# Key and receptance projections in three fp32r passes, a quarter of the value projection moved, rotation tables moved to GpSimd

## What is computed

```python
h = rms_norm(x, norm_g)
dx = jnp.pad(h, ((0, 0), (1, 0), (0, 0)))[:, :-1] - h
xr, xw, xk, xv, xa, xg = (h + dx * mu[i] for i in range(6))
r = xr @ w_r
k = xk @ w_k
v = xv @ w_v
...
o = wkv7_scan(rh, decay, kh, vh, -kk, kk * ah)
mean = jnp.mean(o, axis=-1, keepdims=True)
var = jnp.mean(jnp.square(o - mean), axis=-1, keepdims=True)
o = (o - mean) * lax.rsqrt(var + LNX_EPS)
o = o.reshape(Bn, Sn, Dn) * lnx_g.astype(f32) + lnx_b.astype(f32)
y = (o + bonus.reshape(Bn, Sn, Dn)) * g.astype(f32)
return y.astype(x.dtype) @ w_o, v_first
```

## Time and profile before

| | |
|---|---|
| median of 3 runs | 973.1 us (972.88 to 975.23) |
| the profiled execution | 973.55 us, its span 971.8 us |
| PE busy | 949.0 us (98%), 6740 matmul records |
| weight loads (PEld) | 826.7 us (85%) |
| DVE busy | 675.8 us (70%) |
| ACT busy | 449.0 us (46%) |
| POOL busy | 85.4 us (9%) |
| mean granted PE clock | 0.996 |
| the time mix | from the start to about 285 us of the span |
| first feed-forward layer, attention, second feed-forward layer | to about 478, 754 and 970 us |

### The profile page before, as it was taken

The page is one execution under the profiler, slowest core; times in us unless marked ns, Lnnn a source line. Parts: engine busy times, 40 slices in busy tenths (PEclk is TensorE's granted clock), DMA queues, the critical chain, the costliest instruction groups (busy, mean ns, idle before and its releaser), DMA issues.

```text
span 971.8 us, 17678 instructions
## 1 busy us (share of the span) xinstructions
PE 949.0 (98%) x6740; PEld 826.7 (85%) x6740; DVE 675.8 (70%) x1278; ACT 449.0 (46%) x717; POOL 85.4 (9%) x66
## 2 busy tenths in 40 slices
PE   8999999999999999999998999999999999999998
PEld 6778778787778888888898999999998798888887
DVE  7864766658647666666697788888878666666665
ACT  3323324224224444444446566666666554444442
POOL 0201000001010000000022121122112000000000
PEclk9999999999999999999999999999999999999999
DMA  9410320501514767666377555445544147666661
GB/s 300 141 58 1 113 75 1 174 13 26 150 44 129 198 192 194 194 194 194 107 255 211 149 145 159 134 124 157 144 143 134 23 139 227 184 191 184 187 185 58
DMA packets 195127, 136.85 MB, mean 141 GB/s; under 512 B 7279, under 2 KB 185967, under 8 KB 194941
## 3 DMA queue, kind: packets, MB, share of 16 engines
q1 hardware_dynamic: 195068, 136.03, 47.9%
HBM read 134.96 MB, written 1.05 MB: 140 GB/s over the span
## 4 chain that ended last, share of the span: by engine, by line
PE 62%; issue 24%; DVE 8%; POOL 5%; ACT 1%; DMA 1%; POOLq 0%; SPq 0%; DVEq 0%
PE wide L459 32%; PE bank L459 28%; POOL gsm L1910 4%; DVE work L1354 3%; DVE work L1357 2%; DVE x L1354 1%; DMA x<-in_x 1%; DVE wsp L1354 0%; DVE work L1641 0%; PE bank L482 0%; POOL small L1910 0%; ACT work L1028 0%; PE bank L557 0%; DVE wmix_low L1354 0%; DVE am L1354 0%
## 5 line engine op out<-in xcount | busy, mean ns | idle before, releaser
L459 PE MATMUL bank<-wpj,hkq 128*128 128x384 f32 x1152 | 215.8, 341 | 0.9 <-ACT once L1028 0.5
L459 PEld LDWEIGHTS bank<-wpj,hkq 128*128 128x128 f32 x1152 | 198.8, 189 | 5.1 <-issue 1.5
L459 PE MATMUL wide<-hsp,wsp 128*128 128x256 f32 (+2 forms) x1120 | 193.3, 329 | 0.0
L459 PEld LDWEIGHTS wide<-hsp,wsp 128*128 128x128 f32 x1120 | 172.3, 190 | 23.0 <-DVE hsp L1354 0.6
L1354 DVE TENSOR_TENSOR wsp<-ring,wsp 128x1024 fp32r<-128x1024 f32 (+1 forms) x88 | 150.7, 1752 | 4.2 <-ACT wsp L1028 4.2
L1028 ACT ACTIVATE wsp<-ring 128x1024 fp32r<-128x1024 f32 (+1 forms) x88 | 130.3, 1485 | 20.9 <-PE wide L459 14.0
L1354 DVE TENSOR_TENSOR wpj<-ring,wpj 128x1536 fp32r<-128x1536 f32 x48 | 84.2, 1754 | 21.6 <-ACT wpj L1028 21.6
L459 PE MATMUL bank<-wsp,asp 128*128 128x512 f32 x396 | 98.1, 392 | 0.0
L1910 POOL TENSOR_TENSOR gsm<-gsm,mhalf 128x6 f32<-128x6 f32 (+1 forms) x40 | 63.3, 1616 | 310.9 <-DVE gsm L1833 212.6
L459 PEld LDWEIGHTS bank<-wsp,asp 128*128 128x128 f32 x396 | 71.7, 189 | 13.1
L1028 ACT ACTIVATE wpj<-ring 128x1536 fp32r<-128x1536 f32 x48 | 71.2, 1484 | 22.0 <-PE bank L459 15.5
(11 more groups left out here) (253 smaller groups left out, 1163.2 us busy)
## 6 DMA issues: line engine op xcount, KB each, us to landing
ring<-in_f_w_gu SPq DMA_DIRECT2D x88, 512.0 KB, 5.9
ring<-in_w_kv SPq DMA_DIRECT2D x96, 256.0 KB, 3.5
ring<-in_f_w_down SPq DMA_DIRECT2D x44, 512.0 KB, 3.7
ring<-in_b_w_q SPq DMA_DIRECT2D x48, 256.0 KB, 3.5
wmix<-in_a_w_k SPq DMA_DIRECT2D x4, 1024.0 KB, 7.9
wmix<-in_a_w_r SPq DMA_DIRECT2D x4, 1024.0 KB, 10.0
wmix<-in_a_w_v SPq DMA_DIRECT2D x4, 1024.0 KB, 5.3
wmix<-in_a_w_o SPq DMA_DIRECT2D x4, 1024.0 KB, 5.3
```

What stands on the lines that cost most here:

```text
L459: return pe.matmul(o, a, b, start=start, stop=stop)
```

## The change

- The key projections of groups 1 to 3 and the receptance projections of groups 1 to 3 become three-pass products (`project_parts`). Group 0 keeps float32.
- High parts on ACT: the mixed inputs `xk` and `xr` once in group 0; the key columns (`kw_hi`) and receptance columns (`rw_hi`) in every group with a next one. Low parts on DVE: `xk` and `xr` in two halves each in group 0; in every group with a next one the two halves of the key columns behind levels 1 and 2, and those of the receptance columns behind the last copies of X, ahead of the output weights'.
- PE computes three quarters of the receptances ahead of `turn_output`, and one behind the sums of squares. The second quarter of the values moves from behind the matrices to between `turn_norms` and `product_o`.
- DVE makes `y_lo` ahead of the receptance products (`receptances`). In the last group `gu_lo` moves behind the two copies that PE waits for.
- SP's order: the output rows of a group are loaded behind the next group's receptance columns and ahead of its value columns, so that the key columns no longer stand behind `pe_wo`.
- The rotation tables are made by POOL, behind the inverse roots that it makes for the join, and DVE waits for all 12.
- In `heads`, `mean_squares(1, 0)` goes ahead of `half_lo(p, 5)` on DVE; in the last pair ACT makes `half_hi(p, 5)` and the square ahead of a piece of the output weights.

The diff, without a count (`it * 2` to `it * 6` in `product_o`), context and blank lines; 12 spaces of indentation are taken off:

```diff
@@ -358,29 +358,35 @@
-def load_mix(it):
-    for i, free in ((1, "pe_k"), (0, "pe_r"), (2, "pe_v")):
-        if it is not None:
-            sp.wait_ge(S(free), it)
-        c0 = 0 if it is None else it * 256
-        sp.dma_start(wmix[:, i, :].rearrange("p (k n) -> p k n", k=KT),
-                     cols[i][:, :, bass.ds(c0, 256)]).then_inc(s_wm[i], 16)
-        if it is None and i == 1:
-            load_second(c0)
-            sp.dma_start(cst[:, P:NCONST], ins["const"][:, P:NCONST]).then_inc(s_const, 16)
-    if it is not None:
-        sp.wait_ge(S("pe_z"), it * 2)
-        sp.wait_ge(S("pe_g"), it)
-        load_second(it * 256)
-        sp.wait_ge(S("pe_wo"), it * 4)
-    sp.dma_start(wmix[:, 3, :].rearrange("p (n d) -> p n d", n=2),
-                 wo_rows[0 if it is None else it]).then_inc(s_wm[3], 16)
-load_mix(None)
+def load_columns(i, it):
+    sp.dma_start(wmix[:, i, :].rearrange("p (k n) -> p k n", k=KT),
+                 cols[i][:, :, bass.ds(it * 256, 256)]).then_inc(s_wm[i], 16)
+def load_out(it):
+    sp.dma_start(wmix[:, 3, :].rearrange("p (n d) -> p n d", n=2), wo_rows[it]).then_inc(s_wm[3], 16)
+load_columns(1, 0)
+load_second(0)
+sp.dma_start(cst[:, P:NCONST], ins["const"][:, P:NCONST]).then_inc(s_const, 16)
+load_columns(0, 0)
+load_columns(2, 0)
+load_out(0)
 load_gain(1, ins["f_norm_g"][0])
 for it in range(1, NGRP):
-    load_mix(it)
+    sp.wait_ge(S("pe_k"), it)
+    load_columns(1, it)
+    sp.wait_ge(S("pe_r"), it)
+    load_columns(0, it)
+    if it > 1:
+        sp.wait_ge(S("pe_wo"), it * 4 - 4)
+        load_out(it - 1)
+    sp.wait_ge(S("pe_v"), it)
+    load_columns(2, it)
+    sp.wait_ge(S("pe_z"), it * 2)
+    sp.wait_ge(S("pe_g"), it)
+    load_second(it * 256)
+sp.wait_ge(S("pe_wo"), NGRP * 4 - 4)
+load_out(NGRP - 1)
@@ -596,8 +602,9 @@
             if v == 0:
-                pe.wait_ge(s_wm[1], it * 16 + 32)
-            project(7, 1, xk, "pe_k", [v])
+                pe.wait_ge(S("dve_x_lo"), 2)
+                pe.wait_ge(S("dve_mix_lo"), it * 6 + 2)
+            project_parts(7, 1, kw_hi, (xk_hi, xk_lo), "pe_k", [v])
         else:
@@ -616,13 +623,15 @@
         second_rank(it)
-    pe.wait_ge(s_wm[0], it * 16 + 16)
     if behind:
-        project(4, 0, xr, "pe_r", (0, 1))
+        pe.wait_ge(S("dve_x_lo"), 4)
+        pe.wait_ge(S("dve_mix_lo"), it * 6 - 2)
+        project_parts(4, 0, rw_hi, (xr_hi, xr_lo), "pe_r", (0, 1, 2))
         turn_output(it)
         sums_of_squares()
-        project(4, 0, xr, "pe_r", (2, 3))
+        project_parts(4, 0, rw_hi, (xr_hi, xr_lo), "pe_r", [3])
     else:
+        pe.wait_ge(s_wm[0], 16)
         pe.wait_ge(S("dve_mix"), 1)
@@ -637,6 +646,7 @@
         turn_norms()
+        project(6, 2, xv, "pe_v", [early - 1])
         pe.wait_ge(S("act_sa"), it + 1)
@@ -656,9 +666,6 @@
                         m.then_inc(S("pe_mats"), 1)
-    if behind:
-        project(6, 2, xv, "pe_v", [early - 1])
@@ -1102,6 +1109,10 @@
         A(tg[0:LG - P, 1, :], bank[3][0:LG - P, 0:T], ACT.Sigmoid).then_inc(S("act_lora"), 1)
+        act.wait_ge(S("dve_xk"), 2)
+        A(x_hi[:, 1, :], xk.rearrange("p k t -> p (k t)"), ACT.Copy).then_inc(S("act_x_hi"), 1)
+        act.wait_ge(S("dve_mix"), 1)
+        A(x_hi[:, 0, :], xr.rearrange("p k t -> p (k t)"), ACT.Copy).then_inc(S("act_x_hi"), 1)
     act.wait_ge(S("pe_k"), it + 1)
@@ -1133,11 +1144,17 @@
             A(M[:, 4 * c + h:4 * c + 4:2, 2:4, :], bank[MK[h]].rearrange("p (u m t) -> p u m t", u=2, m=2), ACT.Copy).then_inc(S("act_mats"), 1)
+    if ahead:
+        act.wait_ge(s_wm[1], it * 16 + 32)
+        A(kw_hi, wmix[:, 1, :], ACT.Copy).then_inc(S("act_mix_hi"), 1)
     act.wait_ge(S("pe_v"), it + 1)
...
     A(bPn.rearrange("p n i -> p (n i)"), bank[4][:, 256:512], ACT.Copy).then_inc(S("act_kn"), 1)
+    if ahead:
+        act.wait_ge(s_wm[0], it * 16 + 32)
+        A(rw_hi, wmix[:, 0, :], ACT.Copy).then_inc(S("act_mix_hi"), 1)
     if ahead:
@@ -1330,8 +1347,8 @@
     if B: copy_o(0); copy_p(1, 0); copy_p(1, 1)
+    if X: half_hi(p, 5); square(1, 1)
     if X and not follow: wo_high(4, last + 8)
-    if X: half_hi(p, 5); square(1, 1)
     if X and follow: half_hi(p + 1, 0)
@@ -1548,18 +1565,13 @@
     def low_key_weights(h):
-        dve.wait_ge(S("act_kw_hi"), it + 1)
+        dve.wait_ge(S("act_mix_hi"), it * 3 + 1)
     def low_query_weights():
-        dve.wait_ge(S("act_rw_hi"), it + 1)
+        dve.wait_ge(S("act_mix_hi"), it * 3 + 2)
-    def low_output_weights():
-        dve.wait_ge(S("act_mix_hi"), it * 1 + 1)
@@ -1619,13 +1631,16 @@
         decayed_keys()
-        receptances()
         dve.wait_ge(S("act_y_hi"), it)
         low_part(y_lo[:, :, :], yT[:, :, :], y_hi[:, :, :], "dve_y_lo")
+        receptances()
         unit_keys()
...
         invert_norms()
+        dve.wait_ge(S("act_x_hi"), 1)
+        dve.wait_ge(S("pe_k"), 1)
+        low_half("xk", 0)
         unit_keys()
@@ -1635,6 +1650,7 @@
         q.mark(dve.tensor_copy(pl[:, :, :], par[:, two, lg:lg + 2]))
+        low_half("xk", 1)
     if behind:
@@ -1658,6 +1674,10 @@
             add_output(it, [2, 3])
+        if not behind and c == 0:
+            dve.wait_ge(S("act_x_hi"), 2)
+            dve.wait_ge(S("pe_r"), 1)
+            low_half("xr", 0)
     for l in range(1, LEVELS - 1):
@@ -1676,6 +1696,8 @@
                 m.then_inc(S("dve_U"), 1)
+        if ahead and l in (1, 2):
+            low_key_weights(l - 1)
         if l == 3:
@@ -1686,18 +1708,24 @@
     q.mark(m)
-    if not ahead:
-        gu_lo(0, 0, 0)
     for h in range(2):
...
         dve.tensor_copy(Xc[HD:P, 4 * h:4 * h + 4, :], bank[h][HD:P, 0:256].rearrange("p (u t) -> p u t", u=4)).then_inc(S("dve_X"), 1)
-    if ahead and behind:
-        low_output_weights()
+    if not ahead:
+        gu_lo(0, 0, 0)
+    if not behind:
+        low_half("xr", 1)
+    if ahead:
+        low_query_weights()
+        dve.wait_ge(S("act_mix_hi"), it * 3 + 3)
+        low_half("ow", 0)
+        if behind:
+            low_half("ow", 1)
     dve.wait_ge(S("pe_S"), it + 1)
...
     m.then_inc(S("dve_S"), 1)
-    norm_output(it + 1, 0, None if behind else low_output_weights)
+    norm_output(it + 1, 0, None if behind else lambda: low_half("ow", 1))
 group(0, behind=False)
@@ -1809,17 +1837,7 @@
-dve.wait_ge(s_qkg, 32)
-for w in range(2):
-    for r in range(RT):
-        cosr = C("cos")[:, r * HD:(r + 1) * HD].rearrange("p (o d) -> p o d", o=1)
-        sinr = C("sin")[:, r * HD:(r + 1) * HD].rearrange("p (o d) -> p o d", o=1)
-        tt(rot[:, w, 0, r, :, :], qkg[:, w, :, :], cosr.broadcast_to([P, NG, HD]), ALU.mult)
-        for a, b in ((0, 32), (32, 0)):
-            m = tt(rot[:, w, 1, r, :, a:a + 32], qkg[:, w, :, b:b + 32],
-                   sinr[:, :, a:a + 32].broadcast_to([P, NG, 32]), ALU.mult)
-m.then_inc(S("dve_rot"), 1)
-dve.wait_ge(S("dve_rot"), 1)
+dve.wait_ge(S("pool_rot"), 12)
@@ -1886,8 +1904,8 @@
     if X: half_lo(p, 4)
-    if X: norm_rotate(0, 0); norm_rotate(0, 1); half_lo(p, 5)
-    if X: mean_squares(1, 0); mean_squares(1, 1); norm_rotate(1, 0); norm_rotate(1, 1)
+    if X: norm_rotate(0, 0); norm_rotate(0, 1); mean_squares(1, 0); half_lo(p, 5)
+    if X: mean_squares(1, 1); norm_rotate(1, 0); norm_rotate(1, 1)
     if X and follow: half_lo(p + 1, 0)
@@ -1937,6 +1955,15 @@
 norm_root(2)
+pool.wait_ge(s_qkg, 32)
+for w in range(2):
+    for r in range(RT):
+        cosr = C("cos")[:, r * HD:(r + 1) * HD].rearrange("p (o d) -> p o d", o=1)
+        sinr = C("sin")[:, r * HD:(r + 1) * HD].rearrange("p (o d) -> p o d", o=1)
+        pool.tensor_tensor(rot[:, w, 0, r, :, :], qkg[:, w, :, :], cosr.broadcast_to([P, NG, HD]), ALU.mult).then_inc(S("pool_rot"), 1)
+        for a, b in ((0, 32), (32, 0)):
+            pool.tensor_tensor(rot[:, w, 1, r, :, a:a + 32], qkg[:, w, :, b:b + 32],
+                               sinr[:, :, a:a + 32].broadcast_to([P, NG, 32]), ALU.mult).then_inc(S("pool_rot"), 1)
 with pool.Fori(0, KT) as p:
```

4 lines of the change are left out of this document (1 added, 3 removed).

## The result

The changed kernel takes **962.86 us** (median of 4 runs, 962.29 to 964.07), the kernel before in the same session 974.16 us (4 runs, 972.88 to 975.74): a ratio of 0.9888, 95% interval 0.9875 to 0.990. The prediction was 961.8 us, set against a median of 973.1 us over three executions; with a fourth, taken with the changed kernel, that median is 974.16. One execution of the kernel before (1323 us) and one of `tables_dve` (2347 us), far above the others of their kernels, are left out of medians and ratios here. The profiled execution took 962.29 us, its span is 960.6 us, its mean granted clock 0.998; the span is 11.2 us shorter than before.

The account below looks back on a forecast made before the run. PE was taken as the bound, busy 949.0 of 971.8 us. Group boundaries 8.3, group 3 2.1 and heads 0.9 sum to 11.3 us off 973.55, 962.25; against the median 961.8 us, range 958 to 968.

Parts of the forecast that it names:

- The passes: Key and receptance quarters of groups 1 to 3: 1.44 us instead of 1.76, 24 x 0.32 = 7.7 us of PE work.
- over 1.6: Sign that the forecast is wrong: quarters of the three-pass products taking over 1.6 us in the changed profile.
- weight loads bound the passes: Rival, slower: at 0.19 us a record a quarter takes 2.28 us, giving 976.8 us; chance 0.04.
- The moved quarter: Value quarter in groups 1 to 3: the 1.92 us behind the matrices go; boundaries, with the passes, sum to 8.3 us.
- The gain goes into waits: Rival: ACT's norms, `dve_scaled` or the state's halves hold the matrices back, or the clock falls; 967.2 us, chance 0.22.
- The cover: New DVE halves (16 of 1.22 us) and ACT high parts fit idle times; 0.1 us allowed for group 0.
- Group 3: Moving `gu_lo` behind the two copies frees 0.8 us of gap and 1.3 us of low clock: 2.1 us.
- The last pair: Last pair of heads: DVE's rotations end some 2 us sooner and PE's 0.84 us gap closes, 0.9 us.
- The middle pairs: Pairs 1 to 6 of the heads: no PE gap, so their new order gives nothing.
- Pair 0: First pair of heads: 0 gained, since a transfer behind the output weights holds pair 1; bound of 3.9 us.
- POOL takes DVE's time: Rival: DVE stands still for POOL's table products (7.2 us) and half reaches PE; 965.4 us, chance 0.07.
- The evidence against that rival: Against POOL slowing DVE: DVE's low part beside POOL's long roots took 1.75 us as always.

Follow-up runs that it names:

- tables_dve: The changed kernel with the twelve products of the rotation tables moved back from POOL to DVE: 962.23 us (three executions), ratio 0.9872.
- before_wo_early: The kernel before, with the attention's output weights loaded behind the first feed-forward layer's loads: 971.83 us, ratio 0.9982.
- wo_early: The changed kernel with the attention's output weights (4 MB) loaded behind the first feed-forward layer's loads, no longer between pair 0's and pair 1's: 958.89 us, ratio 0.9842.

## Why the prediction was right, and where it was not

The total was right, 11.3 us off against 11.3 between the medians. Term by term:

- **The passes.** 0.120 us a record was measured as 0.12, and a key quarter's gain of 0.32 us as 1.93 - 1.61 = 0.32. The 1.61 us are just past my own sign of being wrong, "over 1.6": I had left out the switches of shape, about 0.17 us, but float32 pays them as well (1.93, where I had 1.76), so the gain came out. For the receptances 4.38 us were measured for three quarters, against 4.4 expected. The rival that weight loads bound the passes is out: each record has its own load, in 0.12 us. The Trainium skill (TensorE: Matmul & The Clock Gate, "Part 3: Packing small matmuls") says that a weight load overlaps running matmuls only when its row group differs, from which I had estimated 2.6 us a quarter: for these matmuls the trace does not agree. The same section also names a background weight buffer, which would allow what the rows show.
- **The moved quarter.** 1.92 us behind the matrices, measured 1.94 and, put back, 1.96. The wait for the norms was to be 0.5 us and was 0.33; `dve_scaled` "about 10.0, just in time" ended at 10.17, 0.06 ahead of the matrices. From the turned output to the matrices I took 0.1 us less; it was 0.31 in group 1 and 0.42 in group 2. The first boundary measured 3.34 us (from +1.07 to -2.27) against 3.0, the other two together 5.89 (to -8.16) against 5.4. In sum 9.2 us against 8.4. "The gain goes into waits" is out with it.
- **The cover.** The halves behind the levels left DVE 0.92 and 0.39 us of idle time, against about 0.8 and 0.3 from the rows, and the state held nobody. The step that failed is "group 0's halves fall in DVE idles of about their own length; I allow 0.1 us". It measured 0.73. The idle time was as long as assumed to within 0.1 us, but POOL's masks ran beside it: they added 0.39 us to the low part and 0.77 to the second small copy, less some slack. The prediction sets nothing of POOL's timeline beside these halves.
- **Group 3.** The gap 0.86 us (0.8), the clock 1.63 (1.3): 2.5 us against 2.1. The bound of 1.7 was the better value. That term hangs on the execution, though: in `before_wo_early` the same gap brought no low clock, and there it would have been nothing.
- **The last pair.** 0.95 us against 0.9.
- **The middle pairs.** "Pairs 1 to 6 have no PE gap" failed: 0.12 us in each of six, 0.65 us. The view prints no wait that short. The difference shows in the start times alone.
- **Pair 0.** I took 0; it lost 1.24 us. The reason given, that the transfer holds pair 1, was right and is shown by `wo_early`. What failed is that nothing would get worse. The rival "POOL takes DVE's time" did happen, at 0.8 us and not 3.6, and POOL's products, priced at 0.6 us each, took up to 2.1 behind a low part of DVE. That is the 0.81 us; the other 0.43 are the clock: the 24 matmuls behind PE's wait for Vs took 5.97 us, 5.56 before.
- **The evidence against that rival** was the wrong row. DVE's low part did stay at 1.75 us beside POOL's roots of 6 columns, in the timeline of the kernel before:

```profile
499.38 1.75 DVE L1354 TENSOR_TENSOR wpj<-ring,wpj 128x1536 fp32r<-128x1536 f32 x1
```

  That said nothing of products of 192 and 96 columns.

Against the profiled execution the misses are +0.8, -0.6, +0.4, -1.2 and +0.65 us, with 0.34 us of a later start that is no effect of the change. They cancel. The total was nearer than the terms deserve, and the clock, which fell behind pair 0 in this execution and not in others, adds chance of its own: up to 1.6 us.
